# Two of four fp32 weight sums per feed-forward unit moved from VectorE to GpSimd

## What is computed

```python
gu = h @ w_ffn_in                      # 1024 -> 2 x 2816
gate, up = gu[..., :D_FF], gu[..., D_FF:]
x = x + rmsnorm((jax.nn.silu(gate) * up) @ w_ffn_down)      # first block

x = x + 0.5 * swiglu_ffn(rmsnorm(x), w_in, w_out)           # second block, four times
```

## Time and profile before

| | |
|---|---|
| time, median of 2 runs | 2854.7 us (2850.03 to 2859.37) |
| profiled execution, its time | 2859.24 us |
| its span, first to last instruction | 2857.5 us |
| mean granted clock of PE | 0.982 |
| busy: PE, DVE, ACT, POOL | 97%, 71%, 41%, 2% |

### The profile page before, as it was taken

The page is one execution under the profiler, slowest core; times in us unless marked ns, Lnnn a source line. Parts: engine busy times, 40 slices in busy tenths (PEclk is TensorE's granted clock), DMA queues, the critical chain, the costliest instruction groups (busy, mean ns, idle before and its releaser), DMA issues.

```text
span 2857.5 us, 41229 instructions
## 1 busy us (share of the span) xinstructions
PE 2770.9 (97%) x16634; PEld 2455.0 (86%) x16634; DVE 2014.9 (71%) x2953; ACT 1159.5 (41%) x1635; POOL 62.5 (2%) x22
## 2 busy tenths in 40 slices
PE   7999999999989999899999999999999999899998
PEld 7887788888878989789898899987999788689897
DVE  4555555454657969589695797875979588669794
ACT  4333444344333434334343443432434357424342
POOL 0000011111000000000000000000000000000000
PEclk9999999899999999999999999999999999899999
DMA  7223212222432333323322233332332343123332
GB/s 219 89 78 104 99 64 92 77 92 97 157 118 103 116 106 103 119 74 109 114 95 100 81 111 104 104 104 78 100 119 89 119 173 110 59 68 110 104 104 74
DMA packets 262191, 295.38 MB, mean 103 GB/s; under 512 B 6210, under 2 KB 248018, under 8 KB 259342
## 3 DMA queue, kind: packets, MB, share of 16 engines
q1 hardware_dynamic: 257008, 281.53, 29.8%
q10 hardware_dynamic: 5022, 11.57, 1.1%
HBM read 276.30 MB, written 16.78 MB: 103 GB/s over the span
## 4 chain that ended last, share of the span: by engine, by line
PE 87%; DVE 10%; ACT 2%; issue 1%; DMA 0%; ACTq 0%; DVEq 0%; SPq 0%
PE bank L1414 14%; PE bank L1416 14%; PE bank L1415 14%; PE bank L1834 8%; PE bank L1832 8%; PE bank L1833 8%; PE bank L1664 4%; PE bank L1722 2%; PE bank L1994 1%; PE bank L1712 1%; PE bank L1429 1%; PE bank L1430 1%; PE bank L1431 1%; PE bank L1684 1%; PE bank L1683 1%
## 5 line engine op out<-in xcount | busy, mean ns | idle before, releaser
L2087 DVE TENSOR_TENSOR w_lo<-w_raw,w_hi 128x2048 fp32r<-128x2048 f32 (+2 forms) x140 | 306.3, 2190 | 145.3 <-ACT w_hi L826 143.2
L1414 PE MATMUL bank<-hid_hi,w_hi 128*128 128x512 f32 x880 | 343.8, 391 | 0.0
L826 ACT ACTIVATE w_hi<-w_raw 128x2048 fp32r<-128x2048 f32 (+2 forms) x134 | 242.9, 1820 | 245.8 <-PE bank L1416 161.6
L1415 PE MATMUL bank<-hid_lo,w_hi 128*128 128x512 f32 x880 | 342.5, 389 | 0.0
L1416 PE MATMUL bank<-hid_hi,w_lo 128*128 128x512 f32 x880 | 342.5, 389 | 0.0
L1414 PE MATMUL bank<-h_hi,w_hi 128*128 128x512 f32 x784 | 313.3, 400 | 20.5 <-DVE h_lo L2465 17.0
L1416 PE MATMUL bank<-h_hi,w_lo 128*128 128x512 f32 x784 | 308.2, 393 | 0.0
L1415 PE MATMUL bank<-h_lo,w_hi 128*128 128x512 f32 x784 | 308.1, 393 | 0.0
L1414 PEld LDWEIGHTS bank<-h_hi,w_hi 128*128 128x128 f32 x784 | 149.4, 191 | 55.6 <-issue 22.8
L1416 PEld LDWEIGHTS bank<-hid_hi,w_lo 128*128 128x128 f32 x880 | 165.2, 188 | 34.6
L1414 PEld LDWEIGHTS bank<-hid_hi,w_hi 128*128 128x128 f32 x880 | 165.2, 188 | 34.2 <-issue 0.5
(11 more groups left out here) (453 smaller groups left out, 6869.4 us busy)
## 6 DMA issues: line engine op xcount, KB each, us to landing
w_raw<-in_ffn_w_in_dram SPq DMA_DIRECT2D x88, 1024.0 KB, 5.1
w_raw<-in_ffn_w_out_dram SPq DMA_DIRECT2D x32, 1024.0 KB, 4.8
w_raw<-in_w_in_dram SPq DMA_DIRECT2D x28, 1024.0 KB, 5.2
w_raw<-in_w_ffn_in_dram SPq DMA_DIRECT2D x22, 1024.0 KB, 5.1
w_raw<-in_ffn_w_out_dram SPq DMA_DIRECT2D x16, 768.0 KB, 4.3
w_raw<-in_conv_w_pw_dram SPq DMA_DIRECT2D x12, 1024.0 KB, 6.6
phase_taps<-in_conv_dw_phases_dram SPq DMA_DIRECT2D x10, 1152.0 KB, 7.8
w_raw<-in_w_ffn_down_dram SPq DMA_DIRECT2D x8, 1024.0 KB, 4.8
```

The source lines that it names most:

```text
L826: nc.scalar.activation(w_hi[SLOT[u]][:, 0:n], raw[s][:, 0:n], ACT.Copy).then_inc(w_hi_ready, 1)
L1414: nc.tensor.matmul(bank[b][:, 0:n], wh, xh, start=first, stop=False)
L1415: nc.tensor.matmul(bank[b][:, 0:n], wh, xl, start=False, stop=False)
L2087: v.tensor_tensor(w_lo[slot][:, 0:n], raw[s][:, 0:n], w_hi[slot][:, 0:n].bitcast(F32), ALU.subtract).then_inc(w_lo_ready, 1)
```

## The change

The first two sums of each of the 80 fast units, which need only raw quarters, are made on POOL, in a function `first_sums` with the waits that `weight_sums` had (the unit before has its low parts, the unit has landed). DVE makes the other two and waits for both of POOL's. `w_summed` now counts four per unit instead of three. POOL's program gets 32 units before its wait for the pooling mixer, and 48 behind its work there.

```diff
@@ sums_high (ACT)
-                    act.wait_ge(w_summed, W_SUMMED + 3 * QUAD_AT[u] + 3)
+                    act.wait_ge(w_summed, W_SUMMED + 4 * QUAD_AT[u] + 4)
@@ the program of POOL, behind the loop of the attention stage
+            def first_sums(u):
+
+                pool.wait_ge(w_lo_ready, u)
+                pool.wait_ge(w_landed[u % 2], 16 * (u // 2 + 1))
+                nc.gpsimd.tensor_tensor(w_sum[:, 0, :, :], quarter(u % 2, 1, 0), quarter(u % 2, 1, 1), ALU.subtract).then_inc(w_summed, 1)
+                nc.gpsimd.tensor_tensor(w_sum[:, 1, :, :], quarter(u % 2, 1, 0), quarter(u % 2, 0, 0), ALU.subtract).then_inc(w_summed, 1)
+
+            for f in range(2):
+                for u in sorted(QUADS):
+                    if U_FFN[f] <= u < U_FFN[f] + PER_FFN:
+                        first_sums(u)
             pool.wait_ge(band_ready, 4)
             pool.wait_ge(w_lo_ready, U_POOL + 1)
             for u in (U_POOL + 1, U_FFN[2]):
...
+            for f in range(2, 5):
+                for u in sorted(QUADS):
+                    if U_FFN[f] <= u < U_FFN[f] + PER_FFN:
+                        first_sums(u)
@@ weight_sums (DVE)
-                    n = W_SUMMED + 3 * QUAD_AT[u]
-                    dve.wait_ge(w_lo_ready, u)
-                    dve.wait_ge(w_landed[u % 2], 16 * (u // 2 + 1))
-                    a11, a12, a21, a22 = (quarter(u % 2, n_, k) for n_ in range(2) for k in range(2))
+                    n = W_SUMMED + 4 * QUAD_AT[u]
+                    a11, a12 = (quarter(u % 2, 0, k) for k in range(2))
                     s1, s3, s2, s4 = (w_sum[:, m, :, :] for m in range(4))
-                    v.tensor_tensor(s1, a21, a22, ALU.subtract).then_inc(w_summed, 1)
-                    v.tensor_tensor(s3, a21, a11, ALU.subtract)
-                    dve.wait_ge(w_summed, n + 1)
+                    dve.wait_ge(w_summed, n + 2)
                     v.tensor_tensor(s2, a11, s1, ALU.subtract).then_inc(w_summed, 1)
-                    dve.wait_ge(w_summed, n + 2)
+                    dve.wait_ge(w_summed, n + 3)
                     v.tensor_tensor(s4, a12, s2, ALU.subtract).then_inc(w_summed, 1)
```

## The result

The changed kernel took 2938.2 us (median of 2 runs, 2936.3 to 2940.2) against 2854.7: a ratio of 1.031, 95% interval 1.028 to 1.034. A longer series (experiment 10) gave 1.034 (1.033 to 1.035), with 2944.2 us against 2848.6. The forecast was 2965, the range 2915 to 3014.

A forecast was written before the change was run, and what follows sets the result against it. DVE was taken to bound the fast steps, with almost no lead over PE. Delays of 21.75 us a feed-forward part, 109 for five, on a 2857.5 us span gave 2965 us after adjustment to the median, range 2915 to 3014.

The forecast's parts named there:

- What bounds the kernel: In fast steps DVE is slower than PE by 1.2 us; its lead is zero at U6, 0.64 us at U10.
- The price of POOL's instruction: One POOL subtraction of 128x512 takes 1.31 us, bounds 1.19 to 1.55, extrapolated from rows of larger sizes.
- Where the sums follow at once: Sums directly behind `sums_low`: DVE starts s2 at 2.91 us instead of 1.24, 1.67 us later.
- Behind `hidden_low`: Where `hidden_low` precedes the sums, it and POOL's pair take turns: s2 at 4.17 us instead of 2.57, 1.60 later.
- The sum: Delays reaching PE: 13.15 us in part 1, 8.6 in part 2, 21.75 a feed-forward part, 109 for five.
- The slack terms: In part 2, G7's and U7's delays vanish; G8's 0.63 us wait for ACT and 0.64 of lead are deducted.
- (1): POOL and DVE do not take turns at SBUF: 13.9 us a feed-forward part, 70 in all, 2925 us; chance 0.13.
- (2): DVE's relief decides: with POOL's pair hidden, PE's five waits go, 2 us less, 2853 us; no separate chance given.
- its balance: One POOL subtraction of 0.53 us would neither gain nor lose; 0.94 us is the edge of 2%.
- (3): PE's clock falls in new gaps; only each part's last unit pays, up to 15 us, 2980; 0.76 together with the forecast.
- What was to be seen: POOL rows near 1.3 us, DVE idle about 2.9 us, PE waiting some 2.3 us before most units, 60 to 70 times.

The follow-up runs named there:

- experiment 10: The changed kernel itself, run again in a longer series beside the kernel before: 1.034 of it, 2944.2 us.
- experiment 3: The changed kernel with only s3 made on POOL; DVE makes s1, s2 and s4 and does not wait for POOL: 1.011 of the kernel before, 2882 us.
- experiment 4: The kernel before, DVE's program unchanged, with POOL making the two subtractions again into a free place for 12 of 16 units a part: 1.043, 2973 us.
- Experiment 9: The changed kernel with `hidden_low` moved behind DVE's two sums, so that it no longer lies beside POOL's pair: 1.038 of the kernel before, 2959.1 us.
- experiment 7: The changed kernel with POOL's two subtractions cut to half of their values, the rest left out: 1.006 of the kernel before.
- experiment 8: The changed kernel with POOL's two subtractions cut to a quarter of their values, the rest left out: 0.999 of the kernel before.
- experiment 1: The changed kernel with DVE's two sums moved behind the combination of products that follows them: 0.999 of the kernel before, 2847.2 us.

## Why the prediction was right, and what was mis-sized

**What bounds the kernel.** Right. DVE's fast step was the slower one, with no lead at U6 and 0.64 us at U10, and the delays reached PE at once: +10.3 and +6.2 us a part in the profile.

**The price of POOL's instruction.** 1.31 was extrapolated from the earlier trace rows; it is 1.29. The smaller sizes, 0.74 and 0.46, lie 0.03 and 0.05 below the line of the earlier trace rows.

**Where the sums follow at once.** 1.67 us was forecast, 1.42 measured. The start was right (0.07, now 0.08). The end was not: I took SP's 0.22 for DVE, which goes on 0.04 after POOL. That is 0.18 of the 0.25; the rest is two instructions that overlap by 0.04 and are 0.02 shorter each.

**Behind `hidden_low`: the term that was mis-sized.** 1.60 was forecast ("take turns: 1.33 + 2.62 + 0.22"), 0.97 measured. They do take turns, as experiments 3 and 4 show; what was wrong is that each instruction keeps the other out for its whole length. `hidden_low` costs POOL's two instructions 0.38 + 0.44 = 0.82 us here, not 1.33: that is 0.51 of the 0.63. The rest is the handover, 0.10 in this place (994.60 + 1.73 = 996.33 to 996.43) and not 0.22. The earlier trace rows have a trace of it that I passed over: the slowed product ends 0.54 us behind POOL, and alone it takes 0.67. Experiment 9 confirms by itself that `hidden_low` hides part of the pair (0.56 us; 1.42 - 0.97 = 0.45 to the start of s2). The Trainium skill's rule (SBUF — State Buffer, Who interferes with whom) holds for which operands contend. Its wording that a shared port is held for the whole instruction would have given the 1.60, and the rows give less.

**The sum.** With the measured prices, 5 x 1.42 + 3 x 0.97 = 10.0 for part 1 and 4 x 1.42 + 2 x 0.97 - 1.27 = 6.4 for part 2, against 10.3 and 6.2 in the trace; 82 in all in place of 109. The 27 us of difference are 5 x 9 x 0.25 = 11 and 5 x 5 x 0.63 = 16. The slack terms (0.63, 0.64, what vanishes at G7 and U7) held. That 2938 - 2855 is nearly this 82 as well is luck: the profiled execution has another 8.7 us of the clock in its last units, and the two runs of the kernel before were 6 us above the 2848.6 of the longer series, in which the change costs 96 (82.7 in the fast units and 12.2 in the last ones).

**Rivals.** (1) is wrong in its mechanism, since there are turns. Its +70 and the forecast's +110 lie on both sides of the +84 of two runs and the +96 of the longer series, nearer to the one in the first and to the other in the second, so the total alone would not have told the two apart; the slowed rows and experiments 3, 4 and 9 do. (2) fell, but its balance was right: experiments 7 and 8 lie on both sides of it. And its gain was never to be had: with the pair hidden (experiment 1) the kernel's median is 1 us lower, within the interval of no change, because PE is then the bound. (3) happened as described, as a part of the forecast: absorbed in the steps, 1.6 us and more in a last unit, in six of the ten last units of the profiled execution (9 us) and in eight of the repeated one (12 us), of the 15 allowed.

**What was to be seen.** POOL's rows and DVE's waits came as said; a step of 23.3 for 24.3; PE's gaps are 11.67 - 9.64 = 2.0 us for 2.3, and 46 are put down to `sums_low`, not 60 to 70 (by the starts of the units PE is late in 53).

## What to carry to other kernels

A piece moved to another engine must be worked on while the first engine has something else in its queue; ask what stands directly behind the wait, and put an independent piece there (here: the combination, which turned +96 us into zero). The piece put there must not read both its operands from SBUF while GpSimd works, since even with VectorE's instructions unchanged 125 us were lost to GpSimd sums that nobody used (experiment 4). And look first at what the bound would be if the move cost nothing: here PE, so there was nothing to win.

## What the runs showed of the hardware that was not expected

- VectorE and GpSimd subtractions that both read SBUF alternate instruction by instruction, and each keeps the other out for less than its own duration: 0.98 to 1.1 of 1.29 us, and 0.4 to 0.5 of 0.69.
- From GpSimd's end to VectorE's start by semaphore it is 0.03 to 0.04 us in 60 units of the changed kernel and 0.10 in the 20 behind `hidden_low`; from VectorE's end to GpSimd's start it is 0.08 in all 80.
- GpSimd's fp32 subtraction takes 0.46, 0.74, 1.29 and 2.39 us for 128, 256, 512 and 1024 values a partition.
- At a granted clock of 1.00 in both, PE's unit of 84 matmuls takes 9.89 us in the kernel before and 9.52 in one part of experiment 1, a few units behind a wait of 0.9 us; a step of the changed kernel has 19.62 busy for 19.79. The last unit of a part takes 9.64 where PE waited just before it and 9.89 where it did not, five each in the kernel before. The profile names no wait inside such a unit, and I did not find out what makes the difference. The rows, before and then experiment 1:

```profile
967.40:977.29 9.89, 9.89 (x86) 9.89 (x85) 9.68 (x15) 4.70 (x6) 0.00 (x0) 1.00 0.25 83
```

```profile
955.94:965.46 9.52, 9.52 (x86) 9.52 (x85) 8.79 (x12) 4.82 (x6) 2.32 (x3) 1.00 0.34 110
```
